# Last up pair computed in two halves of its inner dimension, with the down operand's loads and splits moved into its first half

## The reference

```python
h2 = rmsnorm_2(x, g_ffn[l])
x = x + jnp.square(jax.nn.relu(h2 @ w_up[l])) @ w_down[l]
```

## Time and profile before

| | us |
|---|---|
| median of 3 runs | 2802.17 (2800.43 to 2805.7) |
| profiled execution, first to last instruction | 2802.3 |
| up pairs on PE | 2160.6 to 2470.0 |
| last up pair | 2450.8 to 2470.0 |
| down steps on PE, first to last matmul's start | 2470.0 to 2791.7 |

### The profile page before, as it was taken

How to read it: one execution, slowest core, us unless ns; L and a number is a source line. 1 busy time by engine, 2 the same in 40 slices (tenths; PEclk the granted TensorE clock), 3 DMA queues, 4 the chain that set the end, 5 groups by cost and what they waited for, 6 DMA issues and landing times.

```text
span 2802.3 us, 38646 instructions
## 1 busy us (share of the span) xinstructions
PE 2707.3 (97%) x13208; PEld 2150.3 (77%) x13208; DVE 1614.1 (58%) x2120; ACT 1189.8 (42%) x1779; POOL 1109.0 (40%) x753
## 2 busy tenths in 40 slices
PE   6999999999999998999999999999999999989998
PEld 4788888787777776878886777777788888868886
DVE  7744443304676776583015555554436766788888
ACT  4211123323555555442236667765434433334442
POOL 1222222121555554212221111211123988858886
PEclk9999999999999999999999999999999999999999
DMA  5333321344211213113330101101443343374442
GB/s 228 128 127 120 120 98 45 103 146 140 76 54 45 82 52 114 59 38 111 121 108 31 38 32 37 38 30 61 150 158 120 128 161 141 136 259 158 159 161 92
DMA packets 102110, 294.74 MB, mean 105 GB/s; under 512 B 9856, under 2 KB 10496, under 8 KB 101504
## 3 DMA queue, kind: packets, MB, share of 16 engines
q1 hardware_dynamic: 102016, 293.56, 29.7%
HBM read 220.12 MB, written 73.40 MB: 105 GB/s over the span
## 4 chain that ended last, share of the span: by engine, by line
PE 60%; issue 25%; POOL 6%; DVE 4%; ACT 3%; DMA 1%; POOLq 0%; SPq 0%; ACTq 0%; DVEq 0%
PE PS L847 27%; PE PS L1331 10%; PE PS L1383 5%; PE PS L1077 5%; POOL WL L2747 3%; PE PS L1049 2%; PE PS L982 2%; PE PS L1011 2%; PE PS L1026 2%; PE PS L1235 2%; POOL dL L2860 1%; PE PS L1216 1%; DVE dM L2679 1%; DVE bC L2296 1%; PE PS L1175 1%
## 5 line engine op out<-in xcount | busy, mean ns | idle before, releaser
L2747 POOL TENSOR_TENSOR WL<-WR,WH 128x1024 fp32r<-128x1024 f32 x147 | 367.7, 2501 | 1359.9 <-ACT WH L1421 1252.6
L847 PE MATMUL PS<-HH,WH 128*128 128x512 f32 x1712 | 546.0, 400 | 19.4 <-POOL WL L2747 5.9
L847 PE MATMUL PS<-HL,WH 128*128 128x512 f32 x1712 | 531.6, 392 | 0.0
L847 PE MATMUL PS<-HH,WL 128*128 128x512 f32 x1712 | 530.0, 391 | 0.0
L847 PEld LDWEIGHTS PS<-HH,WH 128*128 128x128 f32 x1712 | 315.4, 189 | 95.9 <-issue 26.3
L847 PEld LDWEIGHTS PS<-HL,WH 128*128 128x128 f32 x1712 | 323.4, 189 | 69.3
L847 PEld LDWEIGHTS PS<-HH,WL 128*128 128x128 f32 x1712 | 323.2, 189 | 69.3
L1421 ACT ACTIVATE WH<-WR 128x1024 fp32r<-128x1024 f32 x147 | 155.6, 1059 | 324.1 <-PE PS L847 226.6
L2771 POOL TENSOR_TENSOR bB<-bB,bC 128x256 f32<-128x256 f32 (+7 forms) x128 | 191.2, 1504 | 191.1 <-DVE bC L2296 191.1
L2296 DVE TENSOR_TENSOR_SCAN bC<-bN,EPSC 128x256 f32<-128x256 f32 (+7 forms) x128 | 222.7, 1751 | 57.3 <-ACT bN L1607 52.4
L2679 DVE TENSOR_TENSOR dM<-PS,dM 128x512 f32<-128x512 f32 x212 | 136.2, 678 | 1.6 <-PE PS L1383 1.2
(11 more groups left out here) (348 smaller groups left out, 5618.7 us busy)
## 6 DMA issues: line engine op xcount, KB each, us to landing
WR<-wst SPq DMA_DIRECT2D x149, 512.0 KB, 3.4
uRAW<-wst SPq DMA_DIRECT2D x32, 512.0 KB, 4.8
hid<-uT SPq DMA_DIRECT2D x32, 512.0 KB, 2.8
dRAW<-wst SPq DMA_DIRECT2D x64, 256.0 KB, 3.6
HLF<-hid SPq DMA_DIRECT2D x28, 512.0 KB, 8.9
GLF<-hid SPq DMA_DIRECT2D x28, 512.0 KB, 8.1
TMP<-mods SPq DMA_DIRECT2D x24, 512.0 KB, 4.2
MR<-mods SPq DMA_DIRECT2D x24, 512.0 KB, 5.3
```

The lines of the kernel that those rows point to most:

```text
L847: last = pe.matmul(PS[:, dst0 + q:dst0 + q + HALF], l, rr[:, k * S + q:k * S + q + HALF], start=a, stop=z)
L2747: pool.tensor_tensor(WL[slot][:, :], WR0[:, :], WH[slot][:, :].bitcast(F32), ALU.subtract).then_inc(w_lo, 1)
```

## The change

The last up pair (n = 15) is no longer computed product by product. PE runs all seven products over blocks 0 and 1 (HH/HL), raising a new semaphore `up_half` after each, and then all seven over blocks 2 and 3 (GH/GL), raising `up_p`. SP issues the seven `load_right(0, i)` after `up_half` and not after `up_p`, and `load_sums(0)` behind all of them. ACT and DVE make the first pieces' high and low parts before they evict the pair. The last turn, of pair 15, is cut in two: `turn_first` stays in step 0 of the down pass, `turn_second` goes to step 1.

```diff
@@ SP
-            end = 7 * (UPS - 1)
-            sp.wait_ge(up_p, end + 1)
-            load_right(0, 0)
-            store_turned(UPS - 2)
-            for i in range(1, 4):
-                sp.wait_ge(up_p, end + i + 1)
+            for i in range(7):
+                sp.wait_ge(up_half, i + 1)
                 load_right(0, i)
+                if i == 2:
+                    store_turned(UPS - 2)
+            sp.wait_ge(up_p, 7 * (UPS - 1) + 4)
             load_sums(0)
-            for i in range(4, 7):
-                sp.wait_ge(up_p, end + i + 1)
-                load_right(0, i)
             store_halves(UPS - 1)
@@ PE
-            up_pair(UPS - 1)
+            n = UPS - 1
+            for i in range(7):
+                pe.wait_ge(up_hi, 7 * n + (i + 1))
+                pe.wait_ge(up_lo, 7 * n + (i + 1))
+                if i:
+                    pe.wait_ge(up_e, 9 * (n - 1) + U_FREE[i])
+                else:
+                    pe.wait_ge(up_c, n)
+                product(i, (0, 1)).then_inc(up_half, 1)
+            for i in range(7):
+                product(i, (2, 3)).then_inc(up_p, 1)
@@ ACT
-            first_copy(UPS - 1)
-            for i in range(3):
-                down_weights_hi(0, 0, 0, i)
-            unit_hi(48, 0, 0)
-            unit_hi(48, 0, 1)
-            for i in range(3, 5):
-                down_weights_hi(0, 0, 0, i)
-            hidden(UPS - 1, 0)
-            unit_hi(48, 0, 2)
-            unit_hi(48, 0, 3)
-            for i in range(5, 7):
-                down_weights_hi(0, 0, 0, i)
-            unit_hi(48, 0, 4)
-            hidden(UPS - 1, 1)
-            unit_hi(48, 0, 5)
-            unit_hi(48, 0, 6)
+            for i in range(2):
+                down_weights_hi(0, 0, 0, i)
+            for i in range(4):
+                unit_hi(48, 0, i)
+                if i == 1:
+                    down_weights_hi(0, 0, 0, 2)
+            first_copy(UPS - 1)
+            down_weights_hi(0, 0, 0, 3)
+            unit_hi(48, 0, 4)
...
+            unit_hi(48, 0, 6)
+            down_weights_hi(0, 0, 0, 6)
+            hidden(UPS - 1, 0)
+            hidden(UPS - 1, 1)
@@ DVE, up_pair(n, ..., last)
-                    if at == 0 and not first:
+                    if at == 0 and not first and not last:
                         turn_hidden(n - 1, first=second)
...
-                    if at == 0:
-                        down_sum(0, 0, 0, 2, first=True)
-                    if at == 1:
-                        down_sum(0, 0, 0, 5, first=True)
-                    for i in ((), (0, 1), (), (2, 3), (4, 5, 6))[at]:
-                        unit_lo(28, 0, i)
+                    if at in (0, 2):
+                        unit_lo(28, 0, 4 + at // 2)
+                    if at == 4:
+                        unit_lo(28, 0, 6)
...
+                if last:
+                    turn_hidden(n - 1)
+                    down_sum(0, 0, 0, 2, first=True)
+                    down_sum(0, 0, 0, 5, first=True)
+                    for i in range(4):
+                        unit_lo(28, 0, i)
                 dve.wait_ge(up_p, 7 * n + 2)
@@ DVE, down_pass
                     if first and m == 0:
-                        turn_hidden(UPS - 1)
+                        turn_first(UPS - 1)
+                    if first and m == 1:
+                        turn_second(UPS - 1)
                     down_add(t + m, m, 6, first)
```

More of the change, by code:

```diff
@@ L530, in block_kernel @@
         up_p = sem("up_p")
+        up_half = sem("up_half")
         up_c = sem("up_c")
@@ L2009, in _ @@
                     up_pair(2 * i + (1 + m), m, i + 1)
-            first_copy(UPS - 1)
-            for i in range(3):
-                down_weights_hi(0, 0, 0, i)
-            unit_hi(48, 0, 0)
-            unit_hi(48, 0, 1)
-            for i in range(3, 5):
-                down_weights_hi(0, 0, 0, i)
-            hidden(UPS - 1, 0)
-            unit_hi(48, 0, 2)
-            unit_hi(48, 0, 3)
-            for i in range(5, 7):
-                down_weights_hi(0, 0, 0, i)
-            unit_hi(48, 0, 4)
+            for i in range(2):
[4 more added lines that the diff above has]
+                    down_weights_hi(0, 0, 0, 2)
+            first_copy(UPS - 1)
+            down_weights_hi(0, 0, 0, 3)
+            unit_hi(48, 0, 4)
+            down_weights_hi(0, 0, 0, 4)
+            unit_hi(48, 0, 5)
+            down_weights_hi(0, 0, 0, 5)
+            unit_hi(48, 0, 6)
+            down_weights_hi(0, 0, 0, 6)
+            hidden(UPS - 1, 0)
             hidden(UPS - 1, 1)
-            unit_hi(48, 0, 5)
-            unit_hi(48, 0, 6)
             def down_pass(t, half, loads, e, last=False):
@@ L2585, in turn_hidden, with turn_first @@
             def turn_hidden(n, first=False):
+                turn_first(n, first)
+                turn_second(n)
+            def turn_first(n, first=False):
                 lower, upper = slice(0, HALF), slice(HALF, S)
@@ L2593, in turn_hidden, with turn_second @@
                 dve.tensor_tensor(UT[0][:, upper], UQ[1][:, upper], UT[0][:, lower], ALU.subtract).then_inc(up_t, 1)
+            def turn_second(n):
+                lower, upper = slice(0, HALF), slice(HALF, S)
                 dve.tensor_tensor(UT[1][:, lower], UQ[1][:, upper], UQ[0][:, upper], ALU.subtract).then_inc(up_t, 1)
```

## The result

The changed kernel takes 2813.95 us (median of 4, 2811.02 to 2816.2), the kernel before 2801.3 beside it (2799.6 to 2805.7): a ratio of 1.0043, interval 1.0029 to 1.0057. The profiled execution lasts 2814.0 us against 2802.3. So it is slower, by 12.65 us in the medians and 11.7 us in the traces, where the prediction had 11.3.

A forecast was written before the change was run, and what follows sets the result against it. PE, busy 97% of the span, was taken as the bound, with loads waiting for bandwidth. Step 4, product 2 came +10.9 us by DVE or without slow clock, +11.8 by PE; +11.3 was taken: 2813.5 us, range 2807 to 2819.

The forecast's parts named there:

- the sum's larger half: Down step 1: GLF loads queued behind the moved turn's store land late, so step 2's sums start 10.9 us later.
- the sum: The predicted chain of times from the last up pair to step 4, product 2, ending 11.3 us later.
- PE's row of the sum: PE's times up to step 4, product 2: at 2535.7 instead of 2523.94, 11.8 us later.
- Loads: HLF loads before the down pass: HLF 0 lands at 2464.6, HLF 3, behind both uT stores, at 2471.2.
- the rival in which it passes them: HLF 3 need not wait for the two uT stores and lands 2.6 us earlier: 2810.9 us, chance 0.05.
- ACT and PE at step 0: Down step 0: ACT's copy ends at 2472.8, PE starts product 0 at 2472.9 and product 2 at about 2482.
- The moved turn: Step 1: the turn ends at 2507.1, GLF 2 lands 8.5 us later, step 2's sums start at 2519.4.
- who releases step 3: PE's start of step 3: 1.4 us after DVE's step-2 sums, at 2520.8, after some 10 us of idle.
- Half clock: PE's slow clock after the idle before step 3: up to 2.6 us, hardly adding because DVE's row ends close by.
- The covered turn: Rival at the end of step 1: the wait for GLF 2 and 3 costs nothing; +2.1 us, 2804.3, chance 0.12.
- the faster kernel: Rival: HLF loads land as soon as issued, PE's idle goes and the turn is covered; 2797 us, chance 0.05.
- the slower one: Rival: half clock twice on the path, out of step 0 and in step 3; +16.5 us, 2818.7, chance 0.09.

The follow-up runs named there:

- weights only lifted: The changed kernel with the step-3 weights alone moved ahead of both uT stores in SP's queue; 2810.66 us, ratio 1.0041.
- the kernel with early evictions: The changed kernel with the whole turn in step 0, bank 0 copied early, DVE's evictions between its low parts, SP's queue reordered; 2796.86 us, ratio 0.9988.

## Why the prediction was right, point by point

- *The number.* The time, 2813.95 us against 2813.5, came by the mechanism of the sum's larger half: the store of the moved turn holds up what stands behind it in SP's queue. That it is so near is partly luck. The down sums began 1.4 us early, step 3 began 1.0 us late (2521.76, forecast 2520.8) for a load that the sum doesn't have, and step 4's product 2 came 12.4 us late where PE's row of the sum had 11.8.
- *Loads.* HLF 0 landed at 2464.2 (forecast 2464.6) and HLF 3 at 2471.0 (2471.2), behind both uT stores; the rival in which it passes them has fallen. "DMA: Bandwidth & Descriptors" of the Trainium skill, section Queues, rings and completion order, allows a later transfer to finish first. In this trace that happens by hundredths around the moved store (the first step-3 sum landed at 2516.37, GLF 3, issued before it, at 2516.42) and by up to 0.9 us later in the down steps (weights issued at 2697.47 landed at 2704.98, an HLF piece issued at 2696.05 at 2705.91), but not by a whole transfer of 512 KB, 1.3 us.
- *ACT and PE at step 0.* Copy at 2471.95 and product 0 at 2472.68 (2472.9); product 2 at 2481.31 (2482). The two relus took 1.43 and 1.23 us where the sum had 1.75, which is most of why the down sums began at 2484.08 and not 2485.5. What hangs on it came early too: the step-1 sums by 1.4 us, at 2497.85 (2499.3), the end of the turn by 1.0, at 2506.11 (2507.1).
- *The moved turn.* GLF 2 landed 9.0 us after the turn's end where the sum took 8.5 from before; the two errors cancel in part, and the step-2 sums began at 2518.67, 0.7 us before the forecast. The wait of 9.50 us on DVE is just above the 8 to 9 named.
- *The step that failed: who releases step 3.* The sum had PE start 1.4 us after the step-2 sums, which would be 2520.1. It started 1.7 us later, at 2521.76, released by the step-3 weights, which stand behind the same store. The prediction had not followed that load. Without it (weights only lifted) step 3 begins 1.3 us earlier; the rest of the 1.7 us is the 1.4 itself, which was too short: the kernel before took 1.67 us (2508.51 to 2510.18), that run 2.08. The experiments size the weights: 8.2 us by themselves. Mending only what the prediction had named would have kept most of the loss.
- *Half clock.* It came twice, and added little to the end: step 3 began 11.5 us late and took 2.3 us more than at full clock, step 4 began 13.0 us late, and then 1.1 us came back by step 7, since steps 3 and 4 of the kernel before took 10.4 and 10.5 us, waiting for DVE, and these waits are gone behind a later PE. No run has this wait at full clock. An estimate: DVE's step-3 sums began at 2530.27, and the kernel before needed 5.3 us from there to product 2 of step 4 (2518.62 to 2523.94); that gives 2535.6 by DVE, and PE was there at 2536.34, so half clock cost some 0.7 us.
- *The other rivals.* The covered turn fell with DVE's wait of 9.50 us, the faster kernel with the landing of HLF 3 at 2471.0, and the slower one (16.5 us) with an end 11.7 us late in the trace.
- *The turn's own time* was 1.23 and 1.22 us, as taken. The prediction set a rule of "SBUF — State Buffer" of the Trainium skill, section SBUF: two separate sides, against that row: DVE and POOL hold a port pair exclusively, for a whole instruction. The way it was used there was wrong, for the 1.18 us of POOL's split was itself in part a lengthened time: the same split takes 0.73 us in the last of POOL's rows in the same microseconds:

```profile
2502.10 0.74 POOL L2883 TENSOR_TENSOR dL<-dLF,dH 128x256 fp32r<-128x256 f32 x1
...
2503.49 3.23 POOL L2883 TENSOR_TENSOR dL<-dLF,dH 128x256 fp32r<-128x256 f32 x3
2506.68 0.73 POOL L2883 TENSOR_TENSOR dL<-dRAW,dH 128x256 fp32r<-128x256 f32 x1
```

  A split takes 0.74 us beside DVE's additions out of PSUM (2502.10) and 1.08 beside the turn (three in 3.23), and the turn 1.23 instead of 0.68. Both grow, but less than if each waited for the whole of the other: one of each would take 0.68 + 0.74 = 1.42 us, and the two subtractions start 1.15 us apart. The trace fits the rule in its direction and not in full, and no run took POOL away.

## What to carry over

When an operation moves to a later place, follow its DMA into the issuing queue and list everything that is issued behind it, to the first item that nobody needs soon; each of them is late by the whole move, and mending one of several brings little. A two-microsecond operation cost 11 us here only through that list, and nothing once the list was reordered. And a late start that another engine's queue covers (step 0 here) is worth nothing until that queue is shorter too.

## What was not expected of the hardware

The granted clock stayed at 1.00 from the up pairs through step 4 in the kernel with early evictions, whose longest idle of PE there was 2.5 us; in the kernel before it fell after an idle of 3.92 us. Of the 3 us that kernel had gained by step 4, 2.6 would be what half clock cost before, by the prediction's own reckoning; the runs don't separate the two. And the time from a load's issue to its landing is no property of the load: the same step-3 weights (the middle of two loads) took 7.1 us behind ten loads and 5.0 behind four.
